# Expert gate/up products as three fp32r passes, with weights split on chip and a ring of four experts

## The chip, the core and the metric

The program runs on one NeuronCore of a Trainium2 chip. The metric is the device time of one execution in microseconds (us). The kernel before has a median of 3628.93 us over three runs (3625.93 to 3633.09). The trace comes from one profiled execution. Its span, from the first to the last instruction of the engines, is 3593.0 us.

The engines are named as the profile names them: PE is the matrix engine (PEld its loads of the stationary operand), DVE the vector engine, ACT the scalar engine, POOL the general-purpose engine, SP the engine that only issues transfers. "SPq", "ACTq" and "POOLq" are the instruction queues of these engines.

## The reference

One layer of a decoder block on 2048 tokens of width 1024. Only the last part matters here, the mixture of experts:

```python
def expert_block(args):                       # xb: 128 tokens of one expert
    xb, e = args
    gate, up = jnp.split(xb @ w_gate_up[e], 2, axis=-1)     # [1024, 512] per expert
    return (jax.nn.silu(gate) * up) @ w_down[e]             # [256, 1024] per expert
```

There are 64 experts. Each token goes to two experts of one group of eight; the tokens of an expert are put into blocks of 128 rows, each block goes through its expert, and the outputs are added back with routing weights. All arrays are float32. One expert's weights are 2 MB (gate and up) and 1 MB (down).

## The kernel before

The program is a row of stages, each a block of its own with one instruction stream per engine, written by hand, and semaphores between them. The stages are: norm and transpose, input projection (lines 232 to 436, twice, prefixes `pi_` and `pj_`), latents, attention (`at_`), mix (`mx_`), cross-attention (`xa_`), a third norm, `route` (`rt_`), `experts` (`ex_`) and `combine` (`cb_`). A stage begins when the one before has ended on all engines.

`route` works out the expert of every token and writes a table of token numbers per block. While it runs, SP loads the weights of the first two experts (`load_first_experts`, lines 2083 and 2084).

`experts` runs 64 steps. A step of PE (lines 1716 to 1767) is: `gate_up(b)`, eight products of f32 operands (L1731), stationary `xT` 128x128, moving `wg` 128x512, added up in one bank of `psG`; `turn_hidden(b-1)`, two transposes (L1739); `turn(b+1)`, eight transposes of the gathered tokens (L1720); `go_down(b-1)`, four products of f32 operands (L1750). The trace shows each f32 product as two MATMUL records. `psG` and all tiles of a step have two buffers.

ACT and DVE serve that chain in order. ACT: `sigmoid(b)` (L1791), `take_h(b-1)` (L1795), `take_x(b+1)` for one half of the transposed tokens (L1787), `take_y(b-1)` (L1801) and the store of y (L1805, it waits for both halves of y). DVE: two products for `hidden(b)` (L1853, L1855), the other half of `take_x(b+1)` (L1849), the other half of `take_y(b-1)` (L1860).

POOL gathers the tokens of step b+2 (lines 1688 to 1692) once `turn(b)` is done. SP loads weights into two slots. Its order is what matters for the change:

```python
sp.wait_ge(up, n_up)                  # L1666: gate_up of the expert in this slot is done
sp.dma_start(wg[:, s], ...)           # L1667: 2 MB, rows of 2 KB
sp.wait_ge(down, n_down)              # L1668: its go_down is done, one step later
sp.dma_start(wd[:, s], ...)           # L1669: 1 MB, rows of 4 KB
```

The load of gate/up for the next slot stands behind the wait of L1668, so both loads leave SP together, once a step.

Two other stages hold work of the kind that the change adds. The projection splits raw f32 weights on chip: ACT copies to fp32r (L327), DVE subtracts the copy from the raw values (L381), and PE makes three passes of fp32r (L310). It splits its activations in the same way, from a bank of PSUM (L177 and L178 on ACT, L209 on DVE). The mix makes three fp32r passes with a 128x128 stationary and a 128x512 moving operand (L1094), in the order hi·hi, lo·hi, hi·lo for every k. Attention loads `qraw` and `kraw` with rows of 8 KB onto 64 and 32 partitions (L684 to L687, `qraw[0:NOPE, :]` is 64 partitions of 2048 f32). `combine` has POOL work beside DVE instructions with two operands in SBUF (L1937 and L1940 beside L1974 and L1976).

Of the kernel before, what the change touches and what calls it, by code (L numbers as in the profile page):

```python
# [35 lines left out]
EPS = 1e-6  # L36
NEG = -1e30
# [1388 lines left out]
def route(nc, cst, hT, w_r, b_r, tab_d, wts, dest, tab, meta, load_first_experts):  # L1426
# [3 lines left out]
    with ExitStack() as ctx:  # L1430
# [26 lines left out]
        cmp = s_.sb("cmp", [1, 32, E])  # L1457
# [51 lines left out]
        def _(dve):  # L1509
# [102 lines left out]
            link(V.tensor_tensor(cmp[:], cnt[0:1, 1, :].unsqueeze(1).broadcast_to([1, 32, E]), io32, ALU.is_le))  # L1612
            link(V.tensor_reduce(mf[:, 0:32].unsqueeze(2), cmp[:], AX, ALU.add))
# [16 lines left out]
def experts(nc, cst, h_d, w_gu, w_dn, y_d, tab, meta, wg, wd, g_in, d_in):  # L1630

    with ExitStack() as ctx:
# [5 lines left out]
        xT = s_.sb("xT", [P, 2, KD, P])  # L1638
# [10 lines left out]
        ixd, turned, xa, xv, up, sig, gt, hid, hturn, hcopy, down, ya, yv = (s_.sem(n) for n in (  # L1649
            "ixd", "turned", "xa", "xv", "up", "sig", "gt", "hid", "hturn", "hcopy", "down", "ya", "yv"))  # L1650
# [10 lines left out]

        @block.sync
        def _(sp):
            def dyn(e, s, n_up, n_down):

                sp.wait_ge(up, n_up)  # L1666
                sp.dma_start(wg[:, s], w_gu[bass.ds(e, 1)].rearrange("a (k p) n -> p (a k) n", p=P)).then_inc(g_in[s], 16)  # L1667
                sp.wait_ge(down, n_down)  # L1668
                sp.dma_start(wd[:, s], w_dn[bass.ds(e, 1)].rearrange("a (k p) n -> p (a k) n", p=P)).then_inc(d_in[s], 16)  # L1669
# [41 lines left out]
        @block.tensor  # L1711
        def _(pe):
            def turn(b, s, nx, first=False):
                pe.wait_ge(x_in[s], nx)
                if not first:

                    pe.wait_ge(xa, b)
                    pe.wait_ge(xv, b)
# [23 lines left out]
            def go_down(b, s, nw):  # L1742
                pe.wait_ge(d_in[s], nw)
                pe.wait_ge(hcopy, b + 2)

                pe.wait_ge(ya, b + 1)
                pe.wait_ge(yv, b + 1)
                for f in range(2):
                    for k in range(2):
                        mm = nc.tensor.matmul(psY[f][:], hT[:, s, k, :], wd[:, s, k, f * CH:(f + 1) * CH], start=(k == 0), stop=(k == 1))  # L1750
# [3 lines left out]
            gate_up(0, 0, 16)
            turn(1, 1, 16)
            with pe.Fori(0, E // 2 - 1) as t:
                for s in (1, 0):
                    b = 2 * t + (2 - s)
                    prev = 2 * t + (1 - s)
                    gate_up(b, s, 16 * t + 16 * (2 - s), prev)  # L1760
                    turn_hidden(prev, 1 - s)
                    turn(2 * t + (3 - s), 1 - s, 16 * t + 32)
                    go_down(prev, 1 - s, 16 * t + 16)
            gate_up(E - 1, 1, 16 * (E // 2), E - 2)
            turn_hidden(E - 2, 0)
            go_down(E - 2, 0, 16 * (E // 2))
            turn_hidden(E - 1, 1)
            go_down(E - 1, 1, 16 * (E // 2))

            def more(b):  # L1770

                nw = 16 * (b - E) + 16 * (E // 2 + 1)
                turn(b, 0, nw)
                gate_up(b, 0, nw, b)
                turn_hidden(b, 0)
                go_down(b, 0, nw)

            overflow(pe, more)

        @block.scalar  # L1780
        def _(act):
            def take_x(b, s, first=False):
                act.wait_ge(turned, b + 1)
                if not first:

                    act.wait_ge(up, b - 1)
                nc.scalar.copy(xT[:, s, 0:4, :], psX[0][:]).then_inc(xa, 1)  # L1787

            def sigmoid(b, s):
                act.wait_ge(up, b + 1)  # L1790
# [18 lines left out]
            for s in range(2):  # L1809
                act.sem_inc(st[s], 16)  # L1810
            take_x(0, 0, True)
            sigmoid(0, 0)
            take_x(1, 1, True)
            with act.Fori(0, E // 2 - 1) as t:
                for s in (1, 0):
                    prev = 2 * t + (1 - s)
                    sigmoid(2 * t + (2 - s), s)
                    take_h(prev, 1 - s)
                    take_x(2 * t + (3 - s), 1 - s)
                    take_y(prev, 1 - s, 16 * t)  # L1820
            sigmoid(E - 1, 1)
            take_h(E - 2, 0)
            take_y(E - 2, 0, 16 * (E // 2 - 1))
# [5 lines left out]
            def more(b):  # L1829
                take_x(b, 0)  # L1830
# [11 lines left out]
        def _(dve):  # L1842
            V = nc.vector

            def take_x(b, s, first=False):
                dve.wait_ge(turned, b + 1)
                if not first:
                    dve.wait_ge(up, b - 1)
                V.tensor_copy(xT[:, s, 4:8, :], psX[1][:]).then_inc(xv, 1)  # L1849
# [14 lines left out]
            take_x(0, 0, True)  # L1864
            hidden(0, 0)
            take_x(1, 1, True)
            with dve.Fori(0, E // 2 - 1) as t:
                for s in (1, 0):
                    prev = 2 * t + (1 - s)
                    hidden(2 * t + (2 - s), s)  # L1870
                    take_x(2 * t + (3 - s), 1 - s)
                    take_y(prev, 1 - s, 16 * t)
            hidden(E - 1, 1)
            take_y(E - 2, 0, 16 * (E // 2 - 1))
# [127 lines left out]
def program(nc, a, out):  # L2002
# [13 lines left out]
    with ExitStack() as outer:  # L2016
# [53 lines left out]
        with ExitStack() as back:  # L2070
# [5 lines left out]
            wg = b_.sb("wg", [P, 2, KD, 2 * FF])  # L2076
            wd = b_.sb("wd", [P, 2, 2, D])
            g_in = [b_.sem("g_in0"), b_.sem("g_in1")]
            d_in = [b_.sem("d_in0"), b_.sem("d_in1")]

            def load_first_experts(sp):
                for e in range(2):
                    sp.dma_start(wg[:, e], a["w_gate_up"][e].rearrange("(k p) n -> p k n", p=P)).then_inc(g_in[e], 16)
                    sp.dma_start(wd[:, e], a["w_down"][e].rearrange("(k p) n -> p k n", p=P)).then_inc(d_in[e], 16)
# [4 lines left out]
            experts(nc, cst, h_d, a["w_gate_up"], a["w_down"], y_d, tab, meta, wg, wd, g_in, d_in)  # L2089
# [61 lines left out]
```

## Time and profile before

| what | value |
|---|---|
| median of three runs | 3628.93 us |
| span of the profiled execution | 3593.0 us |
| PE busy in the span | 2972.0 us (83%) |
| DVE, ACT, POOL busy | 1176.3, 968.0, 576.5 us |
| moved by transfers | 514.39 MB, mean 143 GB/s |
| first gate_up of the experts begins | 2584.09 us |
| second gate_up begins | 2595.00 us |
| last gate_up begins | 3476.44 us |
| combine begins | 3498.14 us |

A row of the groups by line reads: line, engine, operation, output<-inputs, shapes, count | busy us, mean ns of one | idle time before them and what ended it. Matmul records overlap, so a run of them is costed by the distance of their starts, or by busy time over count, not by the length of one. A row of the timeline reads: start us, length us, engine, line, operation, count of instructions merged into it, and in brackets the idle time before it and what ended that. In rows of the stretches each engine has its busy time and count; then come the granted clock of TensorE as a share of its higher level, the busy share of the transfer engines, and GB/s. The share can pass 1 by a few hundredths.

### The profile page before, as it was taken

Reading aid. Unit: us, or ns where it says so; the run is one execution under the profiler, and the core shown is the slowest. Engines: PE = TensorE matmul, PEld = TensorE weight load, DVE = VectorE, ACT = ScalarE, POOL = GpSimd, SP = SyncE. Lnnn points to the kernel's source line nnn. Section 1 sums busy time; section 2 is a strip of 40 time slices with the busy share of each in tenths; the row PEclk is TensorE's granted clock in tenths of the full one; section 3 lists DMA queues with packets and bytes.
Section 4 is the critical chain, followed back from the end, with each engine's and each line's share of the span. In section 5 each row is a group of like instructions: output and inputs, shape, how many; then the busy total and the mean of one; then the engine's idle time right before and its main releaser. Section 6 shows DMA issues by size and latency. Waiting matters only on the chain. (4 is left out here: it accounts for less than half of the span.)

```text
span 3593.0 us, 35744 instructions
## 1 busy us (share of the span) xinstructions
PE 2972.0 (83%) x11685; PEld 1958.1 (54%) x11685; DVE 1176.3 (33%) x1718; ACT 968.0 (27%) x1867; POOL 576.5 (16%) x632
## 2 busy tenths in 40 slices
PE   6999699997688889859999599965288888988870
PEld 5888588873266666648998444432144444434430
DVE  4221322104555556534443322335111111111116
ACT  3123311324256565651110321121011111111113
POOL 0000000000145444442221000000400010100005
PEclk8999799998789999979999799976599999989995
DMA  2112311223411211044443551234177887777869
GB/s 104 58 70 93 112 51 59 93 82 113 124 31 32 51 35 30 10 128 133 130 130 93 208 213 47 82 137 166 33 261 263 282 294 281 280 266 268 279 240 365
DMA packets 218280, 514.39 MB, mean 143 GB/s; under 512 B 35648, under 2 KB 64576, under 8 KB 216672
## 3 DMA queue, kind: packets, MB, share of 16 engines
q1 hardware_dynamic: 194144, 446.40, 37.0%
q0 software_dynamic: 14848, 33.60, 2.7%
q10 hardware_dynamic: 9216, 33.56, 2.3%
q8 instruction: 31, 0.51, 0.1%
q14 instruction: 41, 0.34, 0.0%
HBM read 406.00 MB, written 124.13 MB: 148 GB/s over the span
## 5 line engine op out<-in xcount | busy, mean ns | idle before, releaser
L1731 PE MATMUL ex_psG<-ba_wg,ex_xT 128*128 128x512 f32 x1024 | 512.3, 658 | 111.4 <-DMA ba_wg<-in_w_gate_up 109.1
L1731 PEld LDWEIGHTS ex_psG<-ba_wg,ex_xT 128*128 128x128 f32 x1024 | 214.0, 212 | 403.7 <-issue 400.1
L945 POOL TENSOR_TENSOR at_pl<-at_pf,at_ph 128x512 fp32r<-128x512 f32 (+1 forms) x160 | 187.9, 1176 | 319.7 <-ACT at_ph L849 319.7
L1750 PE MATMUL ex_psY<-ba_wd,ex_hT 128*128 128x512 f32 x512 | 230.5, 593 | 2.0 <-ACT ex_hT L1795 1.5
L1853 DVE TENSOR_TENSOR ex_sg<-ex_psG,ex_sg 128x256 f32<-128x256 f32 x64 | 27.1, 424 | 597.8 <-ACT ex_sg L1791 597.8
L846 ACT ACTIVATE at_pf<-at_psS 128x512 f32<-128x512 f32 (+1 forms) x320 | 172.6, 539 | 185.7 <-PE at_psS L755 134.0
L878 DVE TENSOR_REDUCE at_nm<-at_psA 128x1 f32<-128x512 f32 (+2 forms) x320 | 183.9, 607 | 106.0 <-PE at_psA L790 64.1
L908 DVE TENSOR_TENSOR at_pl<-at_pf,at_ph 128x512 fp32r<-128x512 f32 (+2 forms) x160 | 152.0, 959 | 156.3 <-ACT at_ph L849 154.8
L1791 ACT ACTIVATE ex_sg<-ex_psG 128x256 f32<-128x256 f32 x64 | 24.5, 384 | 577.5 <-PE ex_psG L1731 577.5
L1094 PE MATMUL mx_psO<-mx_wo,mx_mT 128*128 128x512 f32 x768 | 175.6, 389 | 0.0
L771 PE MATMUL at_psO<-at_ph,at_vh 128*66 128x512 f32 (+1 forms) x320 | 127.8, 399 | 54.8 <-POOL at_pl L945 44.6
L849 ACT ACTIVATE at_ph<-at_psS 128x512 fp32r<-128x512 f32 (+1 forms) x320 | 171.0, 535 | 0.0
L226 PE MATMUL n_tp<-all_cst,n_xn 128*128 128x128 f32 x384 | 85.2, 396 | 92.9 <-DVE n_xn L198 92.7
L1094 PEld LDWEIGHTS mx_psO<-mx_wo,mx_mT 128*128 128x128 f32 x768 | 143.7, 188 | 29.5
L921 POOL CAST at_vh<-all_cst 128x32 fp32r<-128x32 f32 x2 | 0.5, 229 | 939.0 <-POOLq L442 939.0
L1750 PEld LDWEIGHTS ex_psY<-ba_wd,ex_hT 128*128 128x128 f32 x512 | 92.3, 190 | 94.3 <-issue 94.3
L790 PE MATMUL at_psA<-at_kh,at_qh 96*128 96x512 f32 (+2 forms) x320 | 116.9, 428 | 31.4 <-DVE at_kl L896 27.8
L310 PE MATMUL pi_acc<-hv_hh,pi_wh 128*128 128x512 f32 x512 | 131.4, 399 | 10.7 <-DVE pi_wl L381 10.7
L310 PE MATMUL pj_acc<-hv_hh,pj_wh 128*128 128x512 f32 x512 | 131.4, 399 | 10.3 <-DVE pj_wl L381 10.3
L1688 POOL COPY ex_ix<-ba_tab 128x1 int32 (+1 forms) x64 | 11.4, 178 | 741.8 <-PE ex_psX L1720 741.7
L752 PE MATMUL at_psS<-at_qh,at_kh 98*128 98x512 f32 (+1 forms) x320 | 126.4, 395 | 4.7 <-DMA at_qh<-at_ml 4.7
L310 PE MATMUL pi_acc<-hv_hl,pi_wh 128*128 128x512 f32 x512 | 129.9, 396 | 0.0
(311 smaller groups left out, 5222.6 us busy)
## 6 DMA issues: line engine op xcount, KB each, us to landing
ba_wg<-in_w_gate_up SPq DMA_DIRECT2D x64, 2048.0 KB, 13.1
ba_wd<-in_w_down SPq DMA_DIRECT2D x64, 1024.0 KB, 8.1
y_d<-ex_y ACTq DMA_DIRECT2D x64, 512.0 KB, 7.6
pi_raw<-in_w_slabs SPq DMA_DIRECT2D x32, 512.0 KB, 3.8
pj_raw<-in_w_slabs SPq DMA_DIRECT2D x32, 512.0 KB, 3.8
mx_gt<-gates_d SPq DMA_DIRECT2D x64, 256.0 KB, 5.2
n_xr<-x_d SPq DMA_DIRECT2D x32, 512.0 KB, 5.6
y_d<-xa_zero SPq DMA_DIRECT2D x32, 512.0 KB, 4.8
```

The lines of the kernel that those rows point to most:

```text
L310: mm = nc.tensor.matmul(acc[NCH * s + c][:], w[:, s, k, :], h[:, k, t], start=(i == 0 and k == 0), stop=(i == 2 and k == KD - 1))
L752: nc.tensor.matmul(out, kh[:, s, k], qh[:, s, q], start=True, stop=False)
L771: nc.tensor.matmul(out, vh[:, s, j, :], ph[:, r, off:CH], start=(j == 0), stop=False)
L790: mm = nc.tensor.matmul(psA[b][:, 0:w], qh[0:QKD, s, i * P:(i + 1) * P], kh[0:QKD, s, c * CH:c * CH + w], start=True, stop=not diag)
L846: nc.scalar.activation(pf[:, u % RING, off:CH], psS[u % RING][:, off:CH], ACT.Exp)
L849: nc.scalar.activation(ph[:, u % RING, off:CH], psS[u % RING][:, off:CH], ACT.Exp).then_inc(hi, 1)
L878: V.tensor_reduce(nm[:, i, c:c + 1], psA[b][:, 0:w], AX, ALU.max, negate=True).then_inc(a_max, 1)
L908: V.tensor_tensor(pl[:, r, off:CH], pf[:, r, off:CH], ph[:, r, off:CH], ALU.subtract).then_inc(lo[1], 1)
L945: G_.tensor_tensor(pl[:, r, off:CH], pf[:, r, off:CH], ph[:, r, off:CH], ALU.subtract).then_inc(lo[0], 1)
L1094: mm = nc.tensor.matmul(psO[n][:], mT[:, x_, k, q * P:(q + 1) * P], wop[:, y_, k, hf * CH:(hf + 1) * CH], start=(k == 0 and i == 0), stop= ...
L1731: mm = nc.tensor.matmul(psG[s][:], xT[:, s, k, :], wg[:, s, k, :], start=(k == 0), stop=(k == KD - 1))
L1750: mm = nc.tensor.matmul(psY[f][:], hT[:, s, k, :], wd[:, s, k, f * CH:(f + 1) * CH], start=(k == 0), stop=(k == 1))
```

## The change

Gate/up of an expert is no longer eight f32 products but 24 fp32r products: for each of eight k the three passes hi·hi, hi·lo, lo·hi. For that, ACT copies raw weights to `gh` and DVE writes `gl = raw - gh`; the transposed tokens are split into `xh` (now both halves on ACT) and `xl` (both on DVE). The down product stays f32 and reads the raw tile. The weights of an expert are laid out on the host as three pieces of 1 MB (two of gate/up, one of down), each 128 rows of 8 KB. A tile `raw` holds four experts; the first four are loaded in `route`. In the loop SP loads a piece of gate/up for expert e+4 once `gl` of expert e is written, and the down piece once `go_down(e)` is done. The loops of all engines now have four steps in a turn. A scratch tile of `route` (`cmp`) now lies in another tile's memory.

```diff
@@ route
-        cmp = s_.sb("cmp", [1, 32, E])
+        cmp = lT[0:1, :].rearrange("p (a e) -> p a e", e=E)
@@ experts, SP
-            with sp.Fori(0, E // 2 - 1) as t:
-                for s in range(2):
-                    dyn(2 * t + (s + 2), s, 2 * t + (s + 1), 2 * t + (s + 1))
+            def load(e, r, i):
+                sp.dma_start(raw[:, r, i, :], w_exp[bass.ds(e, 1), i].rearrange("a p n -> p (a n)")).then_inc(r_in[r][i], 16)
+
+            with sp.Fori(0, E // RAW - 1) as t:
+                for r in range(RAW):
+                    e = RAW * t + r
+                    for i in range(2):
+                        sp.wait_ge(w_lo, 2 * e + i + 1)
+                        load(e + RAW, r, i)
+                    sp.wait_ge(down, e + 1)
+                    load(e + RAW, r, 2)
@@ experts, PE
-                for k in range(KD):
-                    mm = nc.tensor.matmul(psG[s][:], xT[:, s, k, :], wg[:, s, k, :], start=(k == 0), stop=(k == KD - 1))
-                mm.then_inc(up, 1)
+                for i in range(2):
+                    pe.wait_ge(x_lo, 2 * b + i + 1)
+                    pe.wait_ge(w_lo, 2 * b + i + 1)
+                    for k in range(KD // 2):
+                        f = i * (KD // 2) + k
+                        nc.tensor.matmul(psG[s][:], xh[:, s, f, :], gh[:, s, i, k, :], start=(f == 0), stop=False)
+                        nc.tensor.matmul(psG[s][:], xh[:, s, f, :], gl[:, s, i, k, :], start=False, stop=False)
+                        mm = nc.tensor.matmul(psG[s][:], xl[:, s, f, :], gh[:, s, i, k, :], start=False, stop=(f == KD - 1))
+                    mm.then_inc(used, 1)
@@ experts, ACT (order of a step b)
+            def weights_high(e, s, r, nw, free=None):
+                for i in range(2):
+                    act.wait_ge(r_in[r][i], nw)
+                    if free is not None:
+                        act.wait_ge(used, 2 * free + i + 1)
+                    nc.scalar.copy(gh[:, s, i], raw[:, r, i, :].rearrange("p (k n) -> p k n", k=KD // 2)).then_inc(w_hi, 1)
 
             def take_x(b, s, first=False):
                 act.wait_ge(turned, b + 1)
-                nc.scalar.copy(xT[:, s, 0:4, :], psX[0][:]).then_inc(xa, 1)
+                for i in range(2):
+                    nc.scalar.copy(xh[:, s, 4 * i:4 * i + 4, :], psX[i][:]).then_inc(x_hi, 1)
+            def step(b, t, j, more):
+                s = j % 2
+                if more:
+                    weights_high(b + 1, 1 - s, (j + 1) % RAW, landed(t, j + 1), b - 1)
+                sigmoid(b, s)
+                take_h(b - 1, 1 - s)
+                if more:
+                    take_x(b + 1, 1 - s)
+                take_y(b - 1, 1 - s, 16 * (RAW // 2) * t + 16 * ((j - 1) // 2))
@@ experts, DVE (order of a step b: weights_low(b+1), hidden(b), take_x(b+1), take_y(b-1))
+            def weights_low(e, s, r):
+                for i in range(2):
+                    dve.wait_ge(w_hi, 2 * e + i + 1)
+                    V.tensor_tensor(gl[:, s, i], raw[:, r, i, :].rearrange("p (k n) -> p k n", k=KD // 2), gh[:, s, i], ALU.subtract).then_inc(w_lo, 1)
 
-                V.tensor_copy(xT[:, s, 4:8, :], psX[1][:]).then_inc(xv, 1)
+                for i in range(2):
+                    dve.wait_ge(x_hi, 2 * b + i + 1)
+                    V.tensor_tensor(xl[:, s, 4 * i:4 * i + 4, :], psX[i][:], xh[:, s, 4 * i:4 * i + 4, :], ALU.subtract).then_inc(x_lo, 1)
@@ program
             def load_first_experts(sp):
-                for e in range(2):
-                    sp.dma_start(wg[:, e], ...)
-                    sp.dma_start(wd[:, e], ...)
+                for e in range(RAW):
+                    for i in range(3):
+                        sp.dma_start(raw[:, e, i, :], a["w_exp"][e, i]).then_inc(r_in[e][i], 16)
```

## Rows read from the trace of the kernel before

**Rows 1.** Timeline, PE: gate_up at the second step, a stalled one, the last.

```profile
2595.00 7.13 PE L1731 MATMUL ex_psG<-ba_wg,ex_xT 128*128 128x512 f32 x16 [1.30 <-DVE ex_xT L1849]
...
2906.81 8.82 PE L1731 MATMUL ex_psG<-ba_wg,ex_xT 128*128 128x512 f32 x16 [3.30 <-DMA ba_wg<-in_w_gate_up]
...
3476.44 7.13 PE L1731 MATMUL ex_psG<-ba_wg,ex_xT 128*128 128x512 f32 x16 [1.26 <-DMA ba_wg<-in_w_gate_up]
```

**Rows 2.** Timeline of a step without a stall, 2920.0 to 2932.6 us.

```profile
2920.00 7.03 PE L1731 MATMUL ex_psG<-ba_wg,ex_xT 128*128 128x512 f32 x16
...
2926.86 0.38 PE L1739 MATMUL ex_psH<-all_cst,ex_hm 128*128 128x128 f32 x2
...
2927.96 3.60 PE L1750 MATMUL ex_psY<-ba_wd,ex_hT 128*128 128x512 f32 x8
2928.16 0.58 ACT L1787 COPY ex_xT<-ex_psX 128x512 f32<-128x512 f32 x1 [0.44 <-PE ex_psX L1720]
...
2931.59 0.58 ACT L1801 COPY ex_y<-ex_psY 128x512 f32<-128x512 f32 x1 [2.85 <-PE ex_psY L1750]
2931.59 0.69 DVE L1860 COPY ex_y<-ex_psY 128x512 f32<-128x512 f32 x1 [2.63 <-PE ex_psY L1750]
...
2932.51 0.41 ACTq L1805 DMA_DIRECT2D y_d<-ex_y  x1
2932.62 0.37 SPq L1667 DMA_DIRECT2D ba_wg<-in_w_gate_up  x1
```

**Rows 3.** Waits over 2584 to 3493: engine line <- releaser: total us, times, longest.

```profile
PE ex_psG L1731 <- DMA ba_wg<-in_w_gate_up: 109.1, 31, 5.1
```

**Rows 4.** Transfers by line, the page: KB each, median us from issue to landing.

```profile
ba_wg<-in_w_gate_up SPq DMA_DIRECT2D x64, 2048.0 KB, 13.1
```

**Rows 5.** Granted clock, transfer share and rate in three stretches of the experts.

```profile
2908.20:2911.60 3.40, 3.40 (x6) 1.33 (x5) 0.00 (x0) 0.00 (x0) 0.00 (x0) 0.50 0.96 381
2917.00:2920.00 3.00, 3.00 (x9) 1.33 (x8) 0.56 (x1) 0.35 (x1) 1.28 (x3) 1.00 0.11 21
2929.00:2932.00 3.00, 2.56 (x6) 0.77 (x5) 0.41 (x1) 0.41 (x1) 1.03 (x1) 1.00 1.05 407
```

**Rows 6.** Transfers by queue, 2700 to 3400 us: packets, MB, share of 16 engines.

```profile
q1 hardware_dynamic: 65022, 155.72, 64.3%
q10 hardware_dynamic: 7200, 26.22, 9.1%
q0 software_dynamic: 7056, 13.12, 5.7%
```

**Rows 7.** Transfers of attention, 941 to 945 us: packets by size.

```profile
DMA packets 142, 0.91 MB, mean 227 GB/s; under 512 B 31, under 2 KB 31, under 8 KB 31
```

**Rows 8.** fp32r products: eight of the projection, and the mix's group by line.

```profile
402.81 2.03 PE L310 MATMUL pi_acc<-hv_hl,pi_wh 128*128 128x512 f32 x8
...
L1094 PE MATMUL mx_psO<-mx_wo,mx_mT 128*128 128x512 f32 x768 | 175.6, 389 | 0.0
```

**Rows 9.** Splits of weights and activations: durations in ns, shortest, median, longest.

```profile
L327 ACT CAST pi_wh<-pi_raw x32: 1039/1049/1053, 42.4 to 383.1; 128x1024 fp32r<-128x1024 f32 x32
L381 DVE TENSOR_TENSOR pi_wl<-pi_raw,pi_wh x32: 1215/1225/1226, 43.5 to 384.1; 128x1024 fp32r<-128x1024 f32 x32
L209 DVE TENSOR_TENSOR hv_hl<-n_tp,hv_hh x32: 678/682/692, 16.1 to 438.6; 128x512 fp32r<-128x512 f32 x32
L1855 DVE TENSOR_TENSOR ex_hm<-ex_psG,ex_sg x64: 423/424/425, 2593.7 to 3484.5; 128x256 f32<-128x256 f32 x64
```

**Rows 10.** Timeline: POOL beside DVE in combine; one gather of the experts.

```profile
3515.41 1.28 DVE L1976 SCALAR_TENSOR_TENSOR cb_xr<-cb_ys,ba_wts,cb_xr 128x1024 f32<-128x1024 f32 x1 [0.16 <-DVE cb_xr L1974]
3515.49 1.25 POOL L1940 TENSOR_TENSOR cb_idle<-cb_idle 1x8 f32<-1x8 f32 x1
...
2929.26 1.03 POOL L1692 DMA_INDIRECT ex_xg<-h_d,ex_ix  x1 [0.53 <-issue]
```

**Rows 11.** Timeline of route: the first scatter into the table.

```profile
2530.25 1.16 POOL L1627 DMA_INDIRECT tab_d<-rt_tok,rt_tp  x1 [78.49 <-DVEq L1617]
```

More of the change, by code:

```diff
@@ L1660, in overflow, with steps, landed @@
                         run(o + E)
+        def steps(eng, step):
+            with eng.Fori(0, E // RAW - 1) as t:
+                for j in range(1, RAW + 1):
+                    step(RAW * t + j, t, j, True)
+            for j in range(1, RAW):
+                step(E - RAW + j, E // RAW - 1, j, j + 1 < RAW)
+        def landed(t, j):
+            return 16 * t + 16 * (j // RAW + 1)
         @block.sync
         def _(sp):
[L1664 to L1669, printed above, removed]
-            with sp.Fori(0, E // 2 - 1) as t:
-                for s in range(2):
-                    dyn(2 * t + (s + 2), s, 2 * t + (s + 1), 2 * t + (s + 1))
+            def load(e, r, i):
[8 more added lines that the diff above has]
+                    load(e + RAW, r, 2)
             def more(b):
                 e = sp.value_load(meta[0:1, bass.ds(b - E, 1)], min_val=0, max_val=E - 1)
-                dyn(e, 0, b, b)
+                sp.wait_ge(down, b)
+                for i in range(3):
+                    load(e, 0, i)
             overflow(sp, more)
@@ L1749, in go_down @@
                     for k in range(2):
[L1750 removed]
+                        mm = nc.tensor.matmul(psY[f][:], hT[:, s, k, :], raw[:, r, 2, k * D + f * CH:k * D + (f + 1) * CH], start=(k == 0), stop=(k == 1))
                 mm.then_inc(down, 1)
             turn(0, 0, 16, True)
[L1754 removed]
+            gate_up(0, 0)
             turn(1, 1, 16)
[L1756 to L1766, printed above, removed]
+            def step(b, t, j, more):
+                s = j % 2
+                gate_up(b, s, b - 1)
+                turn_hidden(b - 1, 1 - s)
+                if more:
+                    turn(b + 1, 1 - s, 16 * (RAW // 2) * t + 16 * ((j + 1) // 2 + 1))
+                go_down(b - 1, 1 - s, (j - 1) % RAW, landed(t, j - 1))
+            steps(pe, step)
             turn_hidden(E - 1, 1)
[L1768 removed]
+            go_down(E - 1, 1, RAW - 1, 16 * (E // RAW))
             def more(b):
[L1772 to L1774 removed]
+                turn(b, 0, 16 * (b - E) + 16 * (E // 2 + 1))
+                gate_up(b, 0, b)
                 turn_hidden(b, 0)
[L1776 removed]
+                go_down(b, 0, 0, 16 * (b - E) + 16 * (E // RAW + 1))
             overflow(pe, more)
@@ L1810, in _, with step @@
                 act.sem_inc(st[s], 16)
+            weights_high(0, 0, 0, 16)
             take_x(0, 0, True)
+            weights_high(1, 1, 1, 16)
             sigmoid(0, 0)
             take_x(1, 1, True)
[L1814 to L1823, printed above, removed]
+            def step(b, t, j, more):
+                s = j % 2
+                if more:
+                    weights_high(b + 1, 1 - s, (j + 1) % RAW, landed(t, j + 1), b - 1)
+                sigmoid(b, s)
+                take_h(b - 1, 1 - s)
+                if more:
+                    take_x(b + 1, 1 - s)
+                take_y(b - 1, 1 - s, 16 * (RAW // 2) * t + 16 * ((j - 1) // 2))
+            steps(act, step)
             take_h(E - 1, 1)
@@ L1863, in _, with step @@
             dve.sem_inc(yv, 1)
-            take_x(0, 0, True)
+            weights_low(0, 0, 0)
+            take_x(0, 0)
+            weights_low(1, 1, 1)
             hidden(0, 0)
[L1866 to L1874, printed above, removed]
+            take_x(1, 1)
+            def step(b, t, j, more):
+                s = j % 2
+                if more:
+                    weights_low(b + 1, 1 - s, (j + 1) % RAW)
+                hidden(b, s)
+                if more:
+                    take_x(b + 1, 1 - s)
+                take_y(b - 1, 1 - s, 16 * (RAW // 2) * t + 16 * ((j - 1) // 2))
+            steps(dve, step)
             take_y(E - 1, 1, 16 * (E // 2 - 1))
             def more(b):
+                weights_low(b, 0, 0)
                 take_x(b, 0)
```

54 lines of the change are left out of this document (25 added, 29 removed).

## The prediction

> **What bounds the kernel now.** The chain that ended last, on the page, reaches back only into `combine`, so it says nothing of the experts. I read the experts' stage itself, in this order: PE's timeline, its waits, the transfers.
>
> PE's gate_up starts at 2595.00 in the second step and at 3476.44 in the last [rows 1]: 881.4 us over 62 steps, 14.22 us a step. A step without a stall takes less [rows 2]: gate_up 2920.00 to 2926.86, 6.86 us; transposes until 2927.96, 1.10 us; go_down is eight records at the same spacing (6.86/16 = 0.429 us), 3.43 us. That is 11.39 us, 706 us for 62 steps. Of the other 175 us, 109.1 are 31 waits for the gate/up load [rows 3]. A second loss hangs on them: after a wait of 3.30 us gate_up takes 8.82 us instead of 7.03 [rows 1, 2], and the granted clock in that step is 0.50, the lower level of 1.2 GHz, for 3.4 us [rows 5]. After a wait of 1.26 us gate_up takes 7.13 us [rows 1], so a short wait costs only itself. At 1.8 us each, up to 31 slow stretches are 55 us, and 164 of the 175 us are explained.
>
> Why is the load late? Not for lack of rate: the transfers fill one stretch at 407 GB/s and rest in another at 21 GB/s [rows 5]. The load leaves SP 1.2 us after the end of go_down [rows 2], is wanted one step later, and needs 13.1 us in the median [rows 4]. The lead is too short, so PE and transfers take turns waiting.
>
> **The change, part by part, for one step.**
>
> *PE.* Removed: 16 f32 records, 6.86 us. Added: 24 fp32r products of the same shape. Eight of the projection take 2.03 us with 0.39 for the last, so (2.03 - 0.39)/7 = 0.234 us each; the mix's 768, which alternate hi and lo as here, take 175.6/768 = 0.229 [rows 8]. I take 0.234: 5.62 us (at 0.229: 5.49). Transposes and go_down stay f32. PE needs 5.62 + 1.10 + 3.43 = 10.15 us a step, 10.02 at least.
>
> The Trainium skill, "FP8 and Floating Point Precision", section TensorE Precision Notes, counts a true FP32 product as four passes. Three passes would then be three quarters of 6.86, 5.14 us, and PE's step 9.67. The rows disagree a little: a pass of f32 is 0.429/2 = 0.214 us, one of fp32r 0.229 to 0.234; the rows decide.
>
> *ACT and DVE.* Added: two copies of 128x2048 on ACT, two subtractions of 128x2048 on DVE, a second half of take_x on both. The nearest rows are half as long. ACT's 1024 columns take 1.049 [rows 9] and 512 take 0.58 [rows 2], so 2048 come to 1.049 + 2 x 0.47 = 1.99, at most 2 x 1.049 = 2.10. DVE: 1.225 for 1024, 0.682 for 512 [rows 9], so 2.31, at most 2.45. DVE's busy time is 2 x 2.31 + 2 x 0.68 + 2 x 0.42 + 0.69 = 7.5 us, under PE's 10.15. But the order is fixed, so I follow it from the end of a go_down, which is the start of the next gate_up, time 0. The store of y leaves ACT at 1.53 (2932.92 - 2931.39) [rows 2]. ACT's first copy ends at 3.52, DVE's two subtractions at 8.14, `hidden` at 8.99, the first half of take_x at 9.67. The next gate_up, at 10.15, needs just that half; the second is needed 2.8 us later. The chain hides under PE with 0.5 us to spare (with the upper lengths it ends at 10.05).
>
> ACT's new wait for raw weights stands ahead of the sigmoid, take_h, take_x and take_y of its step. If it stalls, go_down stalls, and with it the loads queued on SP. What guards it is the lead: SP still issues a step's three pieces behind a go_down, but now for an expert three to four ahead, so a load has two steps and 1.5 us, some 22 us, where it had 10. Nothing is moved past POOL's queue.
>
> *Transfers.* The window 2700 to 3400 has 700/14.22 = 49.2 steps [rows 6]: 3.16 MB of weights, 0.53 of y and 0.27 of gathers each, 3.96 MB. At 407 GB/s [rows 5] that is 9.7 us a step. By the queues' shares it is 79.1% of 14.22, 11.25 us [rows 6]; this counts the slow starts after each rest, so I lean to 407 and take 10.0. The bytes don't change. What 8 KB rows cost no row shows for 128 partitions; 9.7 and 11.25 us are my bounds, and rivals go beyond. The Trainium skill, "DMA: Bandwidth & Descriptors", section Where 436 GB/s comes from, gives about 358 GB/s of HBM for each core; a step would then need 11.1 us. The 407 of this trace stands against it, though over 3 us only.
>
> *The rest.* `route` loads 12.6 MB instead of 6.3, at 0.4 MB/us some 31 us from 2453; the first scatter, which waits for a transfer queued behind them on SP, comes at 2530.25 [rows 11], so it costs nothing (without that cover 16 us). The first split runs while the token table and the first gather come in and ACT and DVE are idle: 0 to 1 us. `cmp` has the same shape as before. The last gate_up saves 1.2 us.
>
> **The sum.** PE 10.15, ACT and DVE 9.7, transfers 10.0 us: three near-equal loads coupled by waits. I add 0.35 us for that, a choice (half to all of the chain's slack lost in a late step): 10.5 us. Short waits leave the clock high [rows 1]. Saved: 62 x (14.22 - 10.5) = 230.6, less about 0 to 1 at the start, plus 1.2 at the end: 231 us. The profiled span goes from 3593.0 to 3362. The runs' median lies 35.9 us above that span; I take this as constant: 3628.93 - 231 = 3398 us. With PE at its least, 10.0, it is 3366; with transfers at 11.25, 3444.
>
> **The rivals.**
> - *Transfers set the step*, at 11.25 us: 62 x 2.97 = 184, 3444 us. For it: the shares of rows 6. Against: 407 GB/s where the queue is full [rows 5], and the deeper ring keeps it full. The skill's 358 GB/s, above, belongs here.
> - *ACT and DVE set it.* POOL's operation on 8 elements lasts 1.25 us, to the end of a 1.28 us DVE instruction with two SBUF operands [rows 10]: they exclude each other. There POOL waits. If DVE also waits for POOL's 1.03 us of a gather, the chain of 10.05 grows to 11.1: 62 x 3.12 = 193, 3435 us; with ACT caught on late raw weights as well, another 0.8 us a step, 3485. Against: DVE's 1.28 is not stretched in that row.
> - *8 KB rows are slow, and the kernel loses.* The only such rows in the trace, 111 of 142 packets, fill the transfer engines at 227 GB/s [rows 7]. At that rate weights need 3.16/0.227 = 13.9 us, with y and gathers (14.8% of 14.22 = 2.1) 16.0 us: 62 x 1.8 = 112 us slower, 3740. It turns at 3.16/(14.22 - 2.1) = 261 GB/s. Against: those transfers write 64 and 32 partitions, and here 128 are written. The Trainium skill, "SBUF — State Buffer", section "Door 1: The DMA port swizzle", has 64 partitions reach half of the ports; by that rule the row says nothing against 128, and its 227 is near half of rows 5's 407.
> - *Three passes cost as much as records of f32*: 24 x 0.429 = 10.3, a step of 14.8, 37 us slower, 3666. Rows 8 speak against it.
>
> **How the numbers follow.** The forecast (steps of 10.0 to 10.9 us, 3366 to 3422) 52%; transfers 22%; ACT and DVE 15%; slow rows 6%; costly passes 2%; something between 12 us and no gain 3%. A measurement of this kernel can tell about 0.2%, 7 us, 0.12 us a step. Faster: 52 + 22 + 15 + 2 = 91%; slower 8%; the same 1%. The range runs from 3366 to 3480, over the transfers and most of the ACT and DVE case; what lies beyond is slow rows, costly passes and most of the in-between, about 12%.
>
> **What would show it.** Right: gate_up starts about 10.5 us apart; 24 records spaced 0.23; waits of PE under 1 us; granted clock near 1.00 through the stage; transfers above 370 GB/s without rests. If transfers win, ACT's copies wait for raw weights and the transfer share stays at 1. If ACT and DVE win, PE waits for `xl` or `gl` while transfers rest, and DVE's subtractions are longer than 2.31 us or sit behind POOL. If 8 KB rows are slow, the share is full at under 261 GB/s. The prediction fails if the coupling of three near-equal loads costs well over 1 us a step, or if a load is late in spite of its lead.

## The result and the profile after

| what | kernel before | kernel after |
|---|---|---|
| median of four runs | 3629.04 us (3625.93 to 3633.09) | 3337.81 us (3336.11 to 3343.39) |
| ratio, 95% interval | | 0.9198 (0.9175 to 0.9221) |
| span of the profiled execution | 3593.0 us | 3334.9 us |
| second gate_up begins | 2595.00 us | 2598.34 us |
| last gate_up begins | 3476.44 us | 3221.91 us |
| one of the 62 steps between | 14.22 us | 10.06 us |
| last gate_up to the end of the span | 116.6 us | 113.0 us |

The direction is as predicted; the time is 60 us below the 3398 of the forecast and 28 us below its range. By the profiled executions 258 us are gone from the 62 steps, 3.3 us are lost ahead of them and 3.6 us won behind them.

The stretches come first. Columns: stretch and its length, busy time and count of PE, PEld, DVE, ACT, POOL, then granted clock, transfer share, GB/s.

```profile
2700.00:2800.00 100.00, 100.00 (x422) 70.70 (x421) 71.41 (x70) 60.19 (x70) 25.01 (x30) 1.00 0.99 392
2700.00:3200.00 500.00, 498.26 (x2091) 351.48 (x2090) 354.83 (x345) 300.25 (x349) 127.62 (x148) 1.00 1.00 391
```

Before, the transfers went at 21 GB/s in one stretch and at 407 in another, and the clock fell to 0.50 [rows 5]. Now PE is busy for 498 of 500 us at a granted clock of 1.00, the higher level of 2.4 GHz, and the transfer share over these 500 us is 1.00 as well, at 391 GB/s. DVE is busy for 71% and ACT for 60%.

One step in the timeline of the kernel after (start, length, engine, line, operation, merged count, and in brackets the idle time before it and what ended it):

```profile
2903.93 0.38 PE L1761 MATMUL ex_psH<-all_cst,ex_hm 128*128 128x128 f32 x2
...
2905.02 3.60 PE L1772 MATMUL ex_psY<-ba_raw,ex_hT 128*128 128x512 f32 x8
...
2905.35 1.23 POOL L1708 COPY ex_ix<-ba_tab 128x1 int32 x1 [6.91 <-PE ex_psX L1739]
...
2907.25 1.28 DVE L1887 TENSOR_TENSOR ex_xl<-ex_psX,ex_xh 128x512 fp32r<-128x512 f32 x2
...
2908.05 0.80 PE L1751 MATMUL ex_psG<-ex_gh,ex_xh 128*128 128x512 f32 x1
...
2908.70 0.39 PE L1752 MATMUL ex_psG<-ex_gl,ex_xh 128*128 128x512 f32 x1
...
2908.74 0.69 DVE L1898 COPY ex_y<-ex_psY 128x512 f32<-128x512 f32 x1 [0.22 <-issue]
...
2909.66 0.34 ACTq L1834 DMA_DIRECT2D y_d<-ex_y  x1
...
2910.12 3.71 ACT L1808 CAST ex_gh<-ba_raw 128x2048 fp32r<-128x2048 f32 x2 [0.81 <-DVE ex_y L1898]
...
2912.06 4.50 DVE L1882 TENSOR_TENSOR ex_gl<-ba_raw,ex_gh 128x2048 fp32r<-128x2048 f32 x2 [2.62 <-ACT ex_gh L1808]
...
2913.93 0.38 PE L1761 MATMUL ex_psH<-all_cst,ex_hm 128*128 128x128 f32 x2
```

From one `turn_hidden` to the next are 2913.93 - 2903.93 = 10.00 us. Transposes take 2905.02 - 2903.93 = 1.09. The 23 products from the second one on take 2913.93 - 2908.70 = 5.23, so 0.2274 each and 5.46 for 24. That leaves 3.45 for go_down. PE shows no gap: the step is PE's own work. The average of the 62 steps, 10.06, is 0.06 us above it.

The waits over 2584 to 3240 us (engine and line <- releaser: total us, times, longest) and the transfers of 2700 to 3200 us by queue (packets, MB, share of 16 engines), with the page's row of the load (count, KB each, median us from issue to landing):

```profile
PE ex_psX L1739 <- DMA ex_xg<-h_d,ex_ix: 76.1, 1, 76.1
...
PEld ex_psG L1751 <- DVE ex_xl L1887: 19.7, 60, 1.8
ACT ex_gh L1808 <- DMA ba_raw<-in_w_exp: 19.1, 25, 1.2
```

```profile
q1 hardware_dynamic: 21389, 155.77, 79.3%
q10 hardware_dynamic: 7179, 26.18, 12.8%
q0 software_dynamic: 7200, 13.54, 7.6%
...
ba_raw<-in_w_exp SPq DMA_DIRECT2D x192, 1024.0 KB, 20.6
```

The first row is PE's one wait for the first gather; it began at 2509 us, while `route` still ran. PE's 109.1 us of waits for the load [rows 3] have no successor on PE: ACT waits 19.1 us for raw weights, and PEld's 60 short waits (0.3 us on average) lie beside PE's work. A piece of 1 MB now takes 20.6 us to land, where a load of 2 MB took 13.1 [rows 4], and is still in time, since it has two steps. Its queue moves 155.77 MB in 79.3% of 500 us, 393 GB/s of full queue (bytes over the time that its packets took); before it was 155.72 MB in 64.3% of 700 us, 346 GB/s [rows 6].

### The profile page after: what moved, and what is told of

The parts are those of the page before. It is cut to its first block and busy times, and to the rows that moved or that the text cites. A ratio compares the mean times of both kernels' runs of the same rounds, so it can differ in the third digit from the quotient of the medians.

```text
span 3334.9 us, 37607 instructions
## 1 busy us (share of the span) xinstructions
PE 2816.0 (84%) x12196; PEld 2030.6 (61%) x12197; DVE 1495.1 (45%) x1910; ACT 1236.6 (37%) x2059; POOL 648.3 (19%) x632
## 5 line engine op out<-in xcount | busy, mean ns | idle before, releaser
L1882 DVE TENSOR_TENSOR ex_gl<-ba_raw,ex_gh 128x2048 fp32r<-128x2048 f32 x128 | 288.4, 2289 | 217.9 <-ACT ex_gh L1808 217.9
L1808 ACT CAST ex_gh<-ba_raw 128x2048 fp32r<-128x2048 f32 x128 | 238.6, 1903 | 136.8 <-PEq L1431 75.1
L1772 PE MATMUL ex_psY<-ba_raw,ex_hT 128*128 128x512 f32 x512 | 231.1, 594 | 3.7 <-issue 2.3
L1751 PE MATMUL ex_psG<-ex_gh,ex_xh 128*128 128x512 f32 x512 | 223.5, 436 | 2.8 <-DVE ex_xl L1887 2.8
L1753 PE MATMUL ex_psG<-ex_gh,ex_xl 128*128 128x512 f32 x512 | 200.4, 391 | 0.0
L1752 PE MATMUL ex_psG<-ex_gl,ex_xh 128*128 128x512 f32 x512 | 200.0, 391 | 0.0
L1708 POOL COPY ex_ix<-ba_tab 128x1 int32 (+1 forms) x64 | 82.2, 1284 | 424.8 <-PE ex_psX L1739 424.7
L1772 PEld LDWEIGHTS ex_psY<-ba_raw,ex_hT 128*128 128x128 f32 x512 | 92.2, 190 | 97.7 <-issue 97.7
L382 DVE TENSOR_TENSOR pi_wl<-pi_raw,pi_wh 128x1024 fp32r<-128x1024 f32 x32 | 39.2, 1225 | 237.3 <-ACT pi_wh L328 237.3
L382 DVE TENSOR_TENSOR pj_wl<-pj_raw,pj_wh 128x1024 fp32r<-128x1024 f32 x32 | 39.2, 1224 | 237.1 <-ACT pj_wh L328 237.0
## 6 DMA issues: line engine op xcount, KB each, us to landing
ba_raw<-in_w_exp SPq DMA_DIRECT2D x192, 1024.0 KB, 20.6
```

Of the source, the lines that this page charges most:

```text
L1751: nc.tensor.matmul(psG[s][:], xh[:, s, f, :], gh[:, s, i, k, :], start=(f == 0), stop=False)
L1752: nc.tensor.matmul(psG[s][:], xh[:, s, f, :], gl[:, s, i, k, :], start=False, stop=False)
L1753: mm = nc.tensor.matmul(psG[s][:], xl[:, s, f, :], gh[:, s, i, k, :], start=False, stop=(f == KD - 1))
L1772: mm = nc.tensor.matmul(psY[f][:], hT[:, s, k, :], raw[:, r, 2, k * D + f * CH:k * D + (f + 1) * CH], start=(k == 0), stop=(k == 1))
L1808: nc.scalar.copy(gh[:, s, i], raw[:, r, i, :].rearrange("p (k n) -> p k n", k=KD // 2)).then_inc(w_hi, 1)
L1882: V.tensor_tensor(gl[:, s, i], raw[:, r, i, :].rearrange("p (k n) -> p k n", k=KD // 2), gh[:, s, i], ALU.subtract).then_inc(w_lo, 1)
```

## The experiments

Three questions are open. Where do the 35.9 us between the span and the median of the kernel before come from? Which part of the change brings how much? And which of PE, transfers and the chain over ACT and DVE is next?

**The kernel before, again (b0).** Theory A: about 36 us lie outside the span. Theory B: the profiled execution of before was a quick one, and the time is the span and little more.

> The kernel before, unchanged. Its runs' median (3629 us) lies 36 us above the span of its profiled execution (3593.0), while after's runs lie 2 us above theirs. Theory A: some 36 us lie outside the span in this kernel; then spans here are about 3593 and times about 3629. Theory B: time and span differ by about 2 us as in after, and the execution profiled first was a quick one; then spans here lie 2 us under the times, at about 3627, and the stalls on the gate/up load are longer than the 109 us of the first profile by some 34 us (with the slow clock that hangs on them).

The median of ten runs is 3626.07 us (3620.09 to 3637.92). The profiled one took 3631.29 with a span of 3629.4. The timeline and the waits (2584 to 3540 us) show where this execution differs from the first profile:

```profile
2594.32 7.13 PE L1731 MATMUL ex_psG<-ba_wg,ex_xT 128*128 128x512 f32 x16 [1.30 <-DVE ex_xT L1849]
...
3514.02 7.13 PE L1731 MATMUL ex_psG<-ba_wg,ex_xT 128*128 128x512 f32 x16 [1.26 <-DMA ba_wg<-in_w_gate_up]
```

```profile
PE ex_psG L1731 <- DMA ba_wg<-in_w_gate_up: 133.0, 31, 6.0
```

The time is the span and 1.9 us; theory A has fallen. The 62 steps take 3514.02 - 2594.32 = 919.7 us, 14.83 each, where the first profile has 14.22 [rows 1]. The 31 waits last 133.0 us instead of 109.1 [rows 3], and PE's gate_up records fill 528.0 us instead of 512.3. The groups by line, the first profile and then this one:

```profile
L1731 PE MATMUL ex_psG<-ba_wg,ex_xT 128*128 128x512 f32 x1024 | 512.3, 658 | 111.4 <-DMA ba_wg<-in_w_gate_up 109.1
L1731 PE MATMUL ex_psG<-ba_wg,ex_xT 128*128 128x512 f32 x1024 | 528.0, 675 | 135.2 <-DMA ba_wg<-in_w_gate_up 133.0
```

The first profiled execution was quicker within the experts alone: 23.9 us of waits and 15.7 us of slower records make up the 38 us between the two. Four runs of before stand beside the result, ten are these, and 20 stood beside the experiments; the quickest of the 34 took 3611.36, still 16 us above that execution's span plus 1.9 us. Why it was quicker no row shows. The 13 other runs that stood beside these ten have a median of 3621.06 us: two sets of runs of one kernel lie 5 us apart, and a difference of that size between two kernels says little.

**A ring of two experts (e1).** Is the depth of the ring what removed the waits?

```diff
-RAW = 4
+RAW = 2
```

> One size changed: the ring holds two experts instead of four; 8 KB rows and fp32r passes stay. Theory (depth is what hides the loads): SP's loads leave at the end of a go_down and are wanted by ACT at once; 3 MB at 0.395 MB/us need some 9.4 us to land, then a copy 1.9, sigmoid and take_h 0.75, go_down 3.4: a step of 15.5 us, up to 18 with PE at the lower clock after the wait, so 3680 to 3835 us, slower than before. Rival (the rate that 8 KB rows give is what counts): step stays near 10.0 us, 3338 us.

Measured: 3983.57 us (3977.64 to 3985.32), ratio 1.0995 (1.0974 to 1.1017): 646 us more than with four, and slower than before. A stretch, the waits of 2700 to 3200 us, and a step:

```profile
2700.00:3200.00 500.00, 307.62 (x1041) 197.09 (x1039) 173.94 (x169) 141.92 (x169) 34.81 (x75) 0.75 0.51 193
```

```profile
ACT ex_gh L1808 <- DMA ba_raw<-in_w_exp: 225.5, 48, 9.1
PE ex_psY L1772 <- issue: 190.2, 24, 8.1
```

```profile
2898.45 5.97 PE L1772 MATMUL ex_psY<-ba_raw,ex_hT 128*128 128x512 f32 x8 [7.96 <-issue]
...
2904.59 1.54 SPq L1681 DMA_DIRECT2D ba_raw<-in_w_exp  x3
...
2913.73 1.90 ACT L1808 CAST ex_gh<-ba_raw 128x2048 fp32r<-128x2048 f32 x1 [8.60 <-DMA ba_raw<-in_w_exp]
...
2916.30 1.90 ACT L1808 CAST ex_gh<-ba_raw 128x2048 fp32r<-128x2048 f32 x1 [0.67 <-DMA ba_raw<-in_w_exp]
...
2918.84 6.02 PE L1772 MATMUL ex_psY<-ba_raw,ex_hT 128*128 128x512 f32 x8 [7.84 <-issue]
```

The transfer share is 0.51: rate is not short, lead is. The circle can be read off. go_down starts at 2898.45; the next load leaves SP at 2904.59, at its end; the copy that waits for it starts at 2913.73; the second copy ends at 2918.20; `take_h` stands behind it on ACT, and go_down starts at 2918.84, 20.4 us after the last one. That the depth decides was right; the price was under-estimated: 15.5 to 18 us a step were expected. The load was right, 9.3 us from the end of go_down to the copy. PE's lower clock was in the upper figure: go_down takes 5.97 us at a granted clock of 0.61, where it took 3.60. What the expectation left out is the second copy: from the start of the first to the end of the second are 4.47 us, where it counted one of 1.9.

**f32 products on the ring of four (e2).** The ring and the 8 KB rows stay, the three passes and the splits go; SP waits for the product itself.

```diff
-                        nc.tensor.matmul(psG[s][:], xh[:, s, f, :], gh[:, s, i, k, :], start=(f == 0), stop=False)
-                        nc.tensor.matmul(psG[s][:], xh[:, s, f, :], gl[:, s, i, k, :], start=False, stop=False)
-                        mm = nc.tensor.matmul(psG[s][:], xl[:, s, f, :], gh[:, s, i, k, :], start=False, stop=(f == KD - 1))
+                        mm = nc.tensor.matmul(psG[s][:], xT[:, s, f, :], raw[:, r, i, k * 2 * FF:(k + 1) * 2 * FF], start=(f == 0), stop=(f == KD - 1))
...
-                        sp.wait_ge(w_lo, 2 * e + i + 1)
+                        sp.wait_ge(used, 2 * e + i + 1)
```

> One part alone: the ring of four with 8 KB rows, but gate/up as f32 products as before (no splits on ACT and DVE, SP waits for the products instead of the subtraction). Theory (the ring takes away waits and slow clock, the passes shorten PE's work): PE's own step of 11.39 us without stalls, so after's time plus 62 x 1.39 = 86 us: 3424 us; of the 291 us gained the ring brings 205. Rival (the loads stay late, only shorter products help): step 14.2 us, 3629 us.

Measured: 3419.41 us (3414.65 to 3425.73), ratio 0.9448 (0.9428 to 0.9468). A stretch, and two starts of `turn_hidden` one step apart:

```profile
2800.00:2900.00 100.00, 100.00 (x301) 49.31 (x300) 19.22 (x36) 16.37 (x36) 12.53 (x27) 1.00 0.93 345
```

```profile
2859.61 0.38 PE L1757 MATMUL ex_psH<-all_cst,ex_hm 128*128 128x128 f32 x2
...
2871.00 0.38 PE L1757 MATMUL ex_psH<-all_cst,ex_hm 128*128 128x128 f32 x2
```

PE is busy throughout at the higher clock, and a step takes 11.39 us, as a step without a stall did before [rows 2]. The gain splits. The kernel before took 3621 us beside these runs and 3626 in b0, so the ring brings 202 to 207 us; the passes bring 3419 - 3338 = 81 us, which is 62 x (11.39 - 10.06) = 82.

**The same with rows of 2 and 4 KB (e8).** The edit of the kernel above and that of the next one together.

> The ring of four alone: f32 products as before, and weights in memory as before, with rows of 2 and 4 KB. Theory (depth alone hides the loads; at 11.4 us a step 375 GB/s are more than the 345 needed): 3419 us as with 8 KB rows. Rival (short rows hold the loads back): transfers at 11.2 us or more come near PE's 11.4, and waits come back: 3430 to 3470 us.

Measured: 3419.93 us (3416.76 to 3421.33), ratio 0.9435 (0.9419 to 0.9451). The load's queue over 2700 to 3200 us, in e2 and here:

```profile
q1 hardware_dynamic: 18957, 138.04, 75.4%
q1 hardware_dynamic: 58319, 137.97, 80.3%
```

The same bytes take more of the queue's time with short rows (344 GB/s of full queue instead of 366), but at 11.4 us a step the length of the rows is worth nothing in the kernel's time; the ring of four hides the loads without them. The ring also brought pieces of 1 MB and another order on SP. e1 has both of these and only half the depth, and stalls, so they are not enough; what they bring beside the depth was not run apart.

**Three passes with rows of 2 and 4 KB (e3).** Are the longer rows needed at all?

```diff
-                sp.dma_start(raw[:, r, i, :], w_exp[bass.ds(e, 1), i].rearrange("a p n -> p (a n)")).then_inc(r_in[r][i], 16)
+                if i < 2:
+                    sp.dma_start(raw[:, r, i, :].rearrange("p (k n) -> p k n", k=KD // 2), w_gu[bass.ds(e, 1), i * (D // 2):(i + 1) * (D // 2), :].rearrange("a (k p) n -> p (a k) n", p=P)).then_inc(r_in[r][i], 16)
+                else:
+                    sp.dma_start(raw[:, r, i, :].rearrange("p (k n) -> p k n", k=2), w_dn[bass.ds(e, 1)].rearrange("a (k p) n -> p (a k) n", p=P)).then_inc(r_in[r][i], 16)
```

> One part undone: the ring of four and the fp32r passes stay, but the weights lie in memory as before, so gate/up comes in rows of 2 KB and down in rows of 4 KB. Theory (PE sets the step, any rate of 390 GB/s is enough): step 10.0 us, 3338 us, transfer share near 1. Rival (the row length makes the rate): weights at the 346 GB/s that the queue's share gave before need 9.1 us, y and gathers 2.1: a step of 11.2 us, 3412 us.

Measured: 3360.59 us (3357.09 to 3365.39), ratio 0.9276 (0.9259 to 0.9294), 23 us above the kernel after. Stretch, waits and the load's queue, 2700 to 3200 us:

```profile
2700.00:3200.00 500.00, 482.06 (x2006) 338.25 (x2004) 339.83 (x331) 284.50 (x332) 125.44 (x142) 1.00 1.01 373
```

```profile
ACT ex_gh L1811 <- DMA ba_raw<-in_w_gate_up: 53.2, 49, 3.3
```

```profile
q1 hardware_dynamic: 62749, 148.55, 81.3%
```

The transfers are full here, at 373 GB/s where the kernel after has 391, and ACT waits 53.2 us for raw weights. The load's queue moves 148.55/(0.813 x 500) = 365 GB/s instead of 393. With short rows the transfers set the step, at 10.4 us; with long ones they stay just under PE's 10.0. The rows are worth 0.37 us a step, between what the two theories gave.

**Two passes (e4).** With PE's load down by a third of gate_up, what is next? The pass hi·lo of the weights is left out, so the product is less exact.

```diff
-                        nc.tensor.matmul(psG[s][:], xh[:, s, f, :], gl[:, s, i, k, :], start=False, stop=False)
```

> One change to the changed kernel: the pass hi x lo of the weights is left out (the product is less exact; ACT, DVE and transfers do all they did), so PE's step falls from 10.0 to 10.0 - 8 x 0.227 = 8.2 us. It tells what comes next behind PE. Theory (transfers: share 0.99 to 1.00 at 392 GB/s): 3.9 MB a step need 9.9 to 10.0 us, so 3330 to 3338 us, no gain. Rival 1 (the chain of ACT and DVE, which in the changed kernel ends 0.54 us before PE needs it): 9.46 us a step, 3304 us. Rival 2 (PE alone): 8.2 us, 3226 us.

Measured: 3330.36 us (3327.82 to 3334.62), ratio 0.9184 (0.9168 to 0.92). PE is rid of 1.8 us a step and the kernel of 7 us in all, not much above the 5 us between two sets of one kernel.

```profile
2700.00:3200.00 500.00, 420.59 (x1673) 274.27 (x1674) 353.98 (x349) 289.48 (x348) 203.13 (x150) 1.00 1.00 391
```

```profile
ACT ex_gh L1807 <- DMA ba_raw<-in_w_exp: 36.7, 46, 1.2
```

PE is busy for 84% only, the transfer share is 1.00 at the rate of the kernel after, and ACT's copies wait for raw weights in 46 of some 50 steps, where 22 did in the kernel after. The transfers are next, at about 9.9 us a step by the medians; its own profile, of the slowest of its four runs, has 10.03 (gate_up at 2598.36 and 62 steps later at 3220.07).

**Two passes with less to load (e6).** The down pieces are loaded for the first four experts alone, and the others compute with those; SP's wait for go_down goes with them, and the pass stays out.

```diff
-                    sp.wait_ge(down, e + 1)
-                    load(e + RAW, r, 2)
...
-                pe.wait_ge(r_in[r][2], nw)
+                pe.wait_ge(r_in[r][2], 16)
```

> Two passes as in the run before, and besides SP loads the down piece for the first four experts only (later ones use those weights again; outputs are not the reference's), so transfers need about 2.9 MB a step, some 7.4 us, and SP waits for no go_down. Theory (with PE and transfers out of the way the chain of ACT and DVE sets the step): 9.46 us, 3304 us. Rival (PE sets it even now): 8.2 us, 3226 us. If the run with two passes and all loads is slower than this one, the difference is what transfers cost there.

Measured: 3321.13 us (3315.89 to 3329.18), ratio 0.9162 (0.9139 to 0.9185). A third of the weights' bytes less gives 9 us, and the 62 steps of the profiles take 605.8 us for e4's 621.7. The stretch, and the circle that is left:

```profile
2700.00:3200.00 500.00, 437.13 (x1736) 281.19 (x1735) 359.52 (x359) 296.32 (x358) 207.53 (x150) 1.00 0.80 285
```

```profile
2905.64 0.68 DVE L1894 COPY ex_y<-ex_psY 128x512 f32<-128x512 f32 x1
...
2907.01 3.71 ACT L1804 CAST ex_gh<-ba_raw 128x2048 fp32r<-128x2048 f32 x2 [0.99 <-DVE ex_y L1894]
...
2908.95 4.49 DVE L1878 TENSOR_TENSOR ex_gl<-ba_raw,ex_gh 128x2048 fp32r<-128x2048 f32 x2 [2.63 <-ACT ex_gh L1804]
...
2914.15 1.28 DVE L1883 TENSOR_TENSOR ex_xl<-ex_psX,ex_xh 128x512 fp32r<-128x512 f32 x2
...
2915.35 0.68 DVE L1894 COPY ex_y<-ex_psY 128x512 f32<-128x512 f32 x1
```

Neither PE (87%) nor the transfers (0.80) are full. ACT's copy waits for DVE's copy of y, since the store of y stands ahead of it on ACT and needs both halves. From one such copy to the next are 2915.35 - 2905.64 = 9.71 us (9.77 on average, with gate_up at 2603.14 and 62 steps later at 3208.95): copy of y, store, ACT's first copy, two subtractions, `hidden`, both halves of take_x, copy of y. The chain over ACT and DVE is the third limit; the expectation had it at 9.46.

**Two more instructions on DVE (e5).** Two subtractions of 128x512 on a scratch tile stand ahead of take_x, all else as after.

```diff
+                    for q in range(2):
+                        V.tensor_tensor(junk[:, q, :], cst[:, 0:512], cst[:, 0:512], ALU.subtract).then_inc(jn, 1)
+                        dve.wait_ge(jn, 2 * b + q - 1)
                     take_x(b + 1, 1 - s)
```

> One cost added to the changed kernel: two DVE instructions of about 0.68 us each on scratch data, ahead of DVE's take_x of every step. Theory (fixed order: the chain store of y, copy, two subtractions, hidden, take_x has 0.54 us to spare before PE needs it): 1.37 - 0.54 = 0.83 us more a step, 62 x 0.83 = 51 us, 3389 us, and PE waits for xl. Rival (DVE is busy 71% of the stage, so 1.4 us a step disappear in its idle time): 3338 us.

Measured: 3417.15 us (3410.66 to 3419.17), ratio 0.9422 (0.9402 to 0.9441), 79 us or 1.28 us a step more. DVE was idle for 29% of the stage, and still nearly the whole of the added 1.41 us shows:

```profile
2904.28 1.41 DVE L1917 TENSOR_TENSOR ex_junk<-all_cst 128x512 f32<-128x512 f32 x2
...
2906.93 0.68 DVE L1900 COPY ex_y<-ex_psY 128x512 f32<-128x512 f32 x1
...
2908.30 3.71 ACT L1810 CAST ex_gh<-ba_raw 128x2048 fp32r<-128x2048 f32 x2 [2.07 <-DVE ex_y L1900]
```

```profile
ACT ex_gh L1810 <- DVE ex_y L1900: 97.3, 44, 2.4
PE ex_psG L1753 <- DVE ex_xl L1889: 43.2, 45, 1.1
```

The circle's average of 9.77 us and 1.41 give 11.18; the steps here are 11.23 apart on average (gate_up at 2603.98 and 62 steps later at 3300.27). The expectation took the slack as 0.54 us; it is 10.00 - 9.77 = 0.23.

## Why the prediction was right, and where it was wrong

The direction, and what removes the waits, were right; two steps of the sum failed. The miss of 60 us has two terms. The first is the base, the time before from which the saving was taken, 33 us; it alone decides that the time lies outside the range. The second is the step, 62 x (10.5 - 10.06) = 27 us. Start and end of the stage cancel to a few tenths.

*The base.* The sum was made against a span of 3593.0, and the step that failed is "The runs' median lies 35.9 us above that span; I take this as constant". It is not constant: the time of a run is its span and 1.9 us, in before and after alike, and the profiled execution was itself a quick one, by 0.61 us a step in the very waits that the change removes. The saving against a typical run is 62 x (14.83 - 10.06) = 296 us; against the quick one it is 258. The median of the kernel after lies only 3337.81 - 3334.9 = 2.9 us above the profiled span. With 2.9 in place of 35.9 the forecast would have been 3365 and its range 3333 to 3447, and the measured time lies in that.

*The coupling.* The second step that failed is "I add 0.35 us for that, a choice". Only 0.06 of it was paid, the average step of 10.06 against PE's own 10.00; the rest is 62 x 0.29 = 18 us. The other 9 us of the step's 27 are PE's sum, 10.15 for 10.00. Three loads of 10.0, 9.9 and 9.8 us run beside each other with next to no gap on PE; loads have two steps of lead and each tile of a step two buffers. Only the longest shows in the time: PE in the kernel after, the transfers in e4, the chain in e6. That the buffers are what absorbs the rest is argued, not measured. PE and the transfers lie so close, within 0.1 us, that the runs hardly part them in the kernel after; PE's 498 of 500 busy us speak for PE.

*PE's step* was the right limit, by the right sum. Of its terms the product was 0.234 and is 0.2274, 0.16 us a step; the mix's 0.229, which alternates hi and lo as here [rows 8], was the nearer row, and the projection's eight records the farther. The least value of the prediction, 10.02, was the one to take. The Trainium skill, "FP8 and Floating Point Precision", section TensorE Precision Notes, counts four passes for a true FP32 product; by an estimate from that a pass would take 6.86/32 = 0.214 us and the passes bring 62 x (6.86 - 5.14) = 107 us. The trace differs: a pass takes 0.227 us, and the passes brought 82.

*The cause of the waits* was right: lead, not rate. e1 has half of the rate unused and is slower than before; the f32 kernels on the ring, with long rows or short, have PE busy for all of 500 us. The low clock went with the waits: 1.00 in the stretches of after and of the f32 kernels, 0.75 in e1.

*Transfers.* Taken as 10.0 us, bounds 9.7 and 11.25. e4, in which they set the step, has it at 10.06 - 7.4/62 = 9.9. The rival at 11.25 has fallen. The prediction put the 346 GB/s of rows 6 down to slow starts after rests. A part of it is the short rows: at like steps they have 344 where 8 KB rows have 366 (e8, e2), and 365 where those have 393 (e3, after). The rest is open: with 8 KB rows the figure is highest where the transfer share is 1.00 (391 in e4, 393 in after), and between 351 (e6, 101.73 MB in 58.0% of 500 us) and 382 (e5, 139.73 in 73.2%) where it is lower. So bytes over a queue's share are no fixed rate to take from one kernel to another. The Trainium skill, "DMA: Bandwidth & Descriptors", section Where 436 GB/s comes from, gives about 358 GB/s of HBM for each core; by an estimate from that a step would take 11.1 us. The 391 GB/s over 500 us stand against it here.

*8 KB rows* do not slow the transfers on 128 partitions: 393 GB/s of full queue, where attention's rows onto 64 and 32 partitions had 227 [rows 7]. The Trainium skill, "SBUF — State Buffer", section "Door 1: The DMA port swizzle", has 64 partitions reach half of the ports that 128 reach; these two rates agree with it roughly. e3 shows what the prediction left open, a gain from them of 23 us.

*ACT and DVE.* The lengths were right: 1.90 and 2.29 us in the groups by line, where 1.99 and 2.31 were taken.

```profile
L1882 DVE TENSOR_TENSOR ex_gl<-ba_raw,ex_gh 128x2048 fp32r<-128x2048 f32 x128 | 288.4, 2289 | 217.9 <-ACT ex_gh L1808 217.9
L1808 ACT CAST ex_gh<-ba_raw 128x2048 fp32r<-128x2048 f32 x128 | 238.6, 1903 | 136.8 <-PEq L1431 75.1
```

The path was not: it was followed from PE's go_down to PE's gate_up, with 0.5 us of slack. It closes without PE, through DVE's copy of y behind the second half of take_x and the store on ACT, and the slack is 0.23. By the prediction's own lengths this circle has none: the second half of take_x ends at 9.67 + 0.68 = 10.35, the copy of y behind the go_down before began at 0.20 (2931.59 - 2931.39) [rows 2], and between them are 10.15 us. That it did not decide here is owed to several lengths a little shorter than taken. The rival "DVE also waits for POOL" has fallen: all 128 subtractions last 2.28 to 2.29 us, with POOL beside them or not.

*The start.* It was put at 0 to 1 us; the second gate_up came 3.3 us later. The timeline of POOL in the kernel after shows a part of the cause, the first gather and a copy behind it, beside DVE's first subtractions:

```profile
2577.80 2.47 POOL L1712 DMA_INDIRECT ex_xg<-h_d,ex_ix  x1 [0.63 <-issue]
2580.28 1.30 POOL L1708 COPY ex_ix<-ba_tab 128x1 int32<-128x1 int32 x1
```

In the kernel before these two took 1.07 and 0.20 us. PE's first transposes wait for that gather, so its 1.4 us lie on the way to the first gate_up. Another 0.7 us were lost before the stage began (POOL's first instruction of it starts at 2574.81 instead of 2574.13); the rest of the 3.3 us was not taken apart.

## What to carry to other kernels

Set the profiled execution's span against the spans of other runs before making a sum on it: where a stage has many waits, as here, one execution can be a per cent quicker than the rest, and the gap to the median then belongs to that stage. Where loads fill only part of the time and the engine still waits for them, count the steps of lead before the rate; the ring was worth some 205 us here, the cheaper products 81. Near-equal loads with two buffers each cost little more than their maximum here, 10.06 us for 10.00, but an engine that is 30% idle may still have under 3% of slack: follow its own order around, through the queues of its neighbours, until it closes.

## What the runs showed of the hardware

- One core moved 391 GB/s over 500 us of mixed traffic (loads, stores of y, gathers), at a share of 1.00. The load's queue ran at 393 GB/s of full queue with rows of 8 KB and at 365 with rows of 2 and 4 KB, 7% less; this shows in the time only in the kernels with three passes, where the transfers are the limit (23 us), and not in the f32 kernels.
- POOL waited for DVE. The copy of 128 words of the token table took 0.20 us at the start of the kernel before and 1.23 in the step shown above, where DVE's two subtractions run beside it and it ends with them; in e1, where it mostly falls into a gap of DVE, it took 0.18 again. The first gather took 1.07 and 2.47. DVE's subtraction kept its 2.29 us; POOL mostly began second, so the runs hardly show whether DVE would wait where POOL begins first. The Trainium skill, "GPSIMD Engine Reference", section Key points, has POOL share its SBUF interfaces with DVE and contend with DVE instructions that have two SBUF inputs; the trace agrees.
- An fp32r product of 128x512 behind its own load of 128x128 took 0.2274 us at a granted clock of 1.00, 6% more than half of one f32 record's 0.429.
- A stalled PE paid twice. In e1 it was busy for 62% of the time at a granted clock of 0.75, and go_down, behind a wait of 7.96 us, took 5.97 us at 0.61 in place of 3.60.
